# Layer norms finished half by half, second-half transposes inside a product, and reordered queues in both blocks

## The chip, the cores and the metric
One core of a Trainium2 chip runs the whole program in one launch. Its engines are TensorE (PE; matmuls and transposes into PSUM), VectorE (DVE), ScalarE (ACT), GpSimd (POOL) and SyncE (SP, here only the issuer of weight loads). Each takes its instructions in the order in which they were written into its own queue, and waits on semaphores of the others. The metric is the device time of one execution in microseconds. A difference of under 0.2% (3.0 us) is about what a measurement of this kernel can't tell from no change.

## The reference
Activations are [256 tokens, 1024 features], float32. Block 1 has two layers, block 2 has one.
```python
for l in range(2):                                     # block 1
    h = hybrid_mixer(x, ...)                 # attentions A and B, gated unit C, three gates, merge
    x = layer_norm(ALPHA * x + h, ln1_g[l], ln1_b[l])
    h = memory_cross_attention(x, mem, x_wq[l], x_wkv[l], x_wo[l])
    x = layer_norm(ALPHA * x + h, ln2_g[l], ln2_b[l])
    h = conv_ffn(x, ...)                     # (gelu(a) * b) @ w_down, a and b convolved over 3 tokens
    x = layer_norm(ALPHA * x + h, ln3_g[l], ln3_b[l])
def layer_norm(x, g, b):
    mu = jnp.mean(xf, axis=-1, keepdims=True)
    var = jnp.mean(jnp.square(xf - mu), axis=-1, keepdims=True)
    y = (xf - mu) * lax.rsqrt(var + LN_EPS) * g + b
```
Block 2 begins with an RMS norm over the same stream. Then come a gated linear recurrence (LRU) whose gate is gelu(x @ w), attention over compressed, selected and nearby keys, where the compressed keys are `gelu(flat @ w1) @ w2` of overlapping blocks ("phi"), and an MLP.

## The kernel before
The 256 tokens lie as two tiles of 128 (`xt(0)`, `xt(1)`, tile name `xs`), one token in a partition. For a product they are turned by PE to features by tokens: `stream_turned(tag, i, src, need, halves)` writes four 128x128 transposes for each half of the features of tile i (line L596) into a PSUM bank. `stream_split` then takes each half out of PSUM as two fp32r numbers, a high part on ACT (L1082, a cast) and a low part, the residue, on DVE (L1644). Both go to `xTr`. A norm's features, halves and tiles are numbered (i, h) below.

All weights are streamed from `d_wst` by SP (L2550) through a ring of four slots (`raw`). Every piece of 1024 columns is split as well: ACT casts the high part to one of six buffers `wh` (L1061) and DVE subtracts for `lows` (L1625). PE makes three products of a piece (high by high, high by low, low by high; L490), in pieces of two feature rows each, so that a 512-wide product of one token tile has four pieces, a = 0, 2, 4 and 6. Pieces 0 and 2 read the first half of the features, 4 and 6 the second.

The order of each queue is written out by hand: `tensor(e)`, and the functions of ACT and DVE, list what they do in the order in which it stands in the queue. On DVE, `lows_for(..., far=n)` also writes the residues of the next n pieces ahead of what follows it.

A layer norm on DVE adds the residual (L1651), takes moments (L1657, L1662), centres and multiplies with the gain in one instruction over 1024 features (`centred`, L1670), then waits for POOL's inverse root `rs` (L2387) and finishes each half (`rooted`, L1680). After a norm, the next product is made by `tokens_by_tile`: `tile(0)` reads tile 0 while the norm of tile 1 runs, and `tile(1)` follows. There are five such places: `up4` (the feed-forward's first columns) in both layers, `kv` (start of layer 1's mixer, behind layer 0's last norm), `q2` (start of block 2, after the RMS norm, whose halves are already scaled separately, L2010) and `mlp4`. The first norm of each layer has no such product: all 16 transposes stand together, and the next product (`xq`) waits for all four residues (`x_ready`).

Other places that the change touches: `gelu_product` (ACT: gelu of a convolved half L1304, then the high part L1307 of its product `z`, which POOL makes, L2464); the fills of the mixer, in which gate and merge products stand between the steps of the attentions (unit `un` 0 to 7; DVE L1891 mixes v, L1863 is a reciprocal of sums, L1815 multiplies a merged product with its gate); and in block 2 the gates `gelu_gate(n)` with their products `ug`, 112 rows each in a piece of 896 columns, between which stand `phi` (L847, weights read from the ring as they are), its transposes (L862), their copy `hid` (DVE L2109) and the product `cmp` that reads it.

## Time and profile before

| | |
|---|---|
| median of 3 runs | 1511.85 us (1511.59 to 1512.86) |
| time of the profiled execution | 1512.52 us |
| its span | 1510.7 us |
| mean granted TensorE clock | 0.999 of full |
| busy: PE, DVE, ACT, POOL | 98%, 68%, 54%, 15% of the span |
| weights moved | 258.17 MB, mean 171 GB/s |

PE is busy in nearly all of the span, so the table says which engine carries the time, but not what a change next to it costs. For that the timeline is read at each place: when PE starts, what ended its wait, and what stands ahead of the releaser in the queue of its engine.

### The profile page before, as it was taken

Reading aid. Unit: us, or ns where it says so; the run is one execution under the profiler, and the core shown is the slowest. Engines: PE = TensorE matmul, PEld = TensorE weight load, DVE = VectorE, ACT = ScalarE, POOL = GpSimd, SP = SyncE. Lnnn points to the kernel's source line nnn. Section 1 sums busy time; section 2 is a strip of 40 time slices with the busy share of each in tenths; the row PEclk is TensorE's granted clock in tenths of the full one; section 3 lists DMA queues with packets and bytes.
Section 4 is the critical chain, followed back from the end, with each engine's and each line's share of the span. In section 5 each row is a group of like instructions: output and inputs, shape, how many; then the busy total and the mean of one; then the engine's idle time right before and its main releaser. Section 6 shows DMA issues by size and latency. Waiting matters only on the chain.

```text
span 1510.7 us, 24653 instructions
## 1 busy us (share of the span) xinstructions
PE 1484.2 (98%) x10055; PEld 1330.5 (88%) x10055; DVE 1023.1 (68%) x1684; ACT 822.3 (54%) x1453; POOL 228.0 (15%) x190
## 2 busy tenths in 40 slices
PE   9999999999999999999999999999999999999999
PEld 6989879799987899988889998789898999899887
DVE  4865686787856676579578774756685697666743
ACT  5577545466642466654556653355446774455632
POOL 2400132211101230022031110104011142100000
PEclk9999999999999999999999999999999999999999
DMA  8633355455564643355454555556321354555453
GB/s 328 240 132 113 112 195 200 159 187 194 172 223 167 223 140 140 98 182 195 140 194 169 191 188 193 195 183 239 114 61 65 115 192 131 198 195 191 173 195 112
DMA packets 40352, 258.17 MB, mean 171 GB/s; under 512 B 4512, under 2 KB 5168, under 8 KB 14000
## 3 DMA queue, kind: packets, MB, share of 16 engines
q1 hardware_dynamic: 35600, 238.44, 45.1%
q0 software_dynamic: 2272, 12.57, 2.3%
q10 hardware_dynamic: 2368, 5.58, 1.0%
q8 instruction: 80, 1.31, 0.3%
q14 instruction: 32, 0.26, 0.1%
HBM read 254.98 MB, written 1.07 MB: 169 GB/s over the span
## 4 chain that ended last, share of the span: by engine, by line
PE 78%; DVE 12%; ACT 7%; DMA 2%; issue 1%; POOL 1%; SPq 0%; ACTq 0%; POOLq 0%; DVEq 0%
PE ps L490 68%; DVE lows L1625 6%; ACT wh L1061 3%; PE ps L596 3%; PE ps L973 1%; DMA raw<-d_wst 1%; PE ps L679 1%; PE ps L694 1%; PE ps L986 1%; ACT arR L1604 1%; DVE S L2361 1%; ACT S L1168 1%; PE ps L768 1%; ACT S L1260 0%; ACT S L1268 0%
## 5 line engine op out<-in xcount | busy, mean ns | idle before, releaser
L1625 DVE TENSOR_TENSOR lows<-raw,wh 128x1024 fp32r<-128x1024 f32 (+3 forms) x473 | 547.4, 1178 | 253.4 <-ACT wh L1061 252.4
L1061 ACT CAST wh<-raw 128x1024 fp32r<-128x1024 f32 (+3 forms) x473 | 455.3, 989 | 174.6 <-DMA raw<-d_wst 141.4
L490 PE MATMUL ps<-xTr,wh 128*128 128x256 f32 (+2 forms) x3472 | 455.1, 284 | 1.6 <-DVE S L1985 1.6
L490 PEld LDWEIGHTS ps<-xTr,wh 128*128 128x128 f32 (+2 forms) x3472 | 430.3, 190 | 5.2 <-DVE S L1985 3.0
L490 PE MATMUL ps<-wh,arR 128*128 128x512 f32 x928 | 290.1, 397 | 0.0
L490 PE MATMUL ps<-xTr,lows 128*128 128x256 f32 (+1 forms) x1736 | 243.6, 283 | 0.0
L490 PEld LDWEIGHTS ps<-xTr,lows 128*128 128x128 f32 (+1 forms) x1736 | 223.2, 190 | 0.4 <-DVE lows L1625 0.2
L490 PEld LDWEIGHTS ps<-wh,arR 128*128 128x128 f32 x928 | 173.8, 188 | 40.1
L490 PE MATMUL ps<-lows,arR 128*128 128x512 f32 x464 | 182.3, 398 | 4.0 <-DVE lows L1625 4.0
L490 PE MATMUL ps<-wh,xTr 128*128 128x512 f32 x480 | 131.1, 394 | 1.6 <-ACT wh L1061 1.1
L490 PE MATMUL ps<-arR,wh 128*128 128x256 f32 (+1 forms) x832 | 111.9, 281 | 1.4 <-DVE ar L1815 1.4
L490 PEld LDWEIGHTS ps<-lows,arR 128*128 128x128 f32 x464 | 87.4, 188 | 29.2 <-DVE lows L1625 9.0
L490 PEld LDWEIGHTS ps<-wh,xTr 128*128 128x128 f32 x480 | 88.7, 188 | 24.1 <-DVE xTr L1644 2.8
L490 PEld LDWEIGHTS ps<-arR,wh 128*128 128x128 f32 (+1 forms) x832 | 103.6, 188 | 3.4 <-DVE ar L1815 2.3
L2387 POOL TENSOR_TENSOR sm<-sm,cst 128x1 f32<-128x1 f32 (+3 forms) x27 | 44.0, 1629 | 370.1 <-DVE sm L1664 243.5
L490 PE MATMUL ps<-lows,xTr 128*128 128x512 f32 x240 | 74.8, 393 | 0.1
L1325 ACT ACTIVATE S<-ps,ar 128x256 f32<-128x256 f32 x88 | 48.5, 561 | 46.1 <-PE ps L490 46.0
L2464 POOL TENSOR_TENSOR S<-S 128x256 f32<-128x256 f32 x44 | 34.2, 778 | 206.1 <-ACT S L1304 206.1
L490 PE MATMUL ps<-arR,lows 128*128 128x256 f32 (+1 forms) x416 | 62.3, 281 | 0.0
L2452 POOL TENSOR_TENSOR ar<-ar 128x256 f32<-128x256 f32 x32 | 28.4, 899 | 201.5 <-DVE ar L1815 201.5
L490 PEld LDWEIGHTS ps<-arR,lows 128*128 128x128 f32 (+1 forms) x416 | 54.6, 188 | 0.6 <-DVE lows L1625 0.6
L490 PEld LDWEIGHTS ps<-lows,xTr 128*128 128x128 f32 x240 | 44.5, 188 | 11.7 <-DVE lows L1625 2.9
(266 smaller groups left out, 1436.8 us busy)
## 6 DMA issues: line engine op xcount, KB each, us to landing
raw<-d_wst SPq DMA_DIRECT2D x196, 1024.0 KB, 4.8
raw<-d_wst SPq DMA_DIRECT2D x24, 512.0 KB, 3.5
raw<-d_wst SPq DMA_DIRECT2D x12, 896.0 KB, 4.6
raw<-d_wst SPq DMA_DIRECT2D x8, 672.0 KB, 4.6
ar<-d_lnp POOLq DMA_DIRECT2D x5, 1024.0 KB, 5.0
raw<-d_wst SPq DMA_DIRECT2D x8, 441.0 KB, 3.5
ar<-d_par POOLq DMA_DIRECT2D x2, 1192.0 KB, 9.6
ar<-d_scr POOLq DMA_DIRECT2D x1, 2048.0 KB, 9.9
```

What stands on the lines that cost most here:

```text
L490: op = e.matmul(out, s, m, start=start and i == 0, stop=stop and i == len(pairs) - 1)
L596: op = e.transpose(o, x, ident[0:x.shape[0], 0:x.shape[0]])
L679: op = e.matmul(bv[64 * g:64 * g + 64, :, :], va[:, k, v:v + 64], PTv[:, hold + g:hold + g + 3:2, k, :], start=(k == 0), stop=(k == 1))
L694: op = e.matmul(bv[:, k, :], qT[br][lo:lo + 64, 2 * hh + k, i * 128:(i + 1) * 128], kT[br][lo:lo + 64, :], start=True, stop=True)
L768: op = e.matmul(b[:, h * 128:(h + 1) * 128], Vx[:, k, h * 128:(h + 1) * 128], PTv[:, 4 * i + h, k, :], start=(k == 0), stop=(k == 1))
L973: op = e.matmul(b[:, h * 65:(h + 1) * 65], PTv[:, hold + h, k, :], vb[:, k, 4 * br + h, :], start=(k == 0), stop=(k == nkt - 1))
L1061: e.copy(high_of(m), raw_of(m)).then_inc(*high.done(m))
L1325: e.activation(hc[:, s, :], M["up", l, m][:, 0:T], ACT.Identity, bias=cb[:, m:m + 1], scale=ck[:, m, 1:2]).then_inc(*act.done("h", l, m))
L1625: e.tensor_tensor(low_of(m), raw_of(m), high_of(m).bitcast(F32), ALU.subtract).then_inc(*low.done(m))
L2387: return e.tensor_tensor(dst, src, mhalf[0:p, 0:n], ALU.pow)
L2452: e.tensor_tensor(merged[:, d, :], merged[:, d, :], gates[:, gate_at[n] + d, :], ALU.add).then_inc(*pool.done("merged", l, n, d))
L2464: e.tensor_tensor(hc[:, s, :], hc[:, s, :], hc[:, s + 1, :], ALU.mult).then_inc(*pool.done("z", l, n))
```

## The change
The second of the two functions `centred` and `rooted` goes, and so does the first: `scaled_half(tag, i, h)` centres, waits for the root and finishes one half of 512 features, then the other. In the five places that run by tiles, the transposes of tile 1's first half stand before `tile(1)` and those of the second half inside it, before piece a = 4. The feed-forward's `z` parts are written one step later. In the mixer, the mixing of v (unit 0) comes ahead of one more residue, and in unit 7 a gated product comes before the reciprocal. In block 2, one more gate stands between each of phi's steps, and the streamed pieces are grouped accordingly.
```diff
@@ tokens_by_tile
-                def tile(i, turn=None):
+                def tile(i, turn=None, at=6):
                     for a, (x, (wH, wL)) in zip(range(0, 8, 2), xs4):
-                        if turn and a == 6:
+                        if turn and a == at:
                             turn()
@@ up4; the same at kv and, with `scaled`, at q2
                 tile(0)
-                stream_turned(tag, 1, xt(1), normed)
+                stream_turned(tag, 1, xt(1), normed, (0,))
                 product.also("stock", l, 2)
-                tile(1)
+                tile(1, turn=lambda: stream_turned(tag, 1, xt(1), normed, (1,)), at=4)
@@ mlp4
-            tile(0, turn=lambda: stream_turned(tag, 1, xn[1], scaled))
+            tile(0, turn=lambda: stream_turned(tag, 1, xn[1], scaled, (0,)))
             product.also("stock", 2, 2)
-            tile(1)
+            tile(1, turn=lambda: stream_turned(tag, 1, xn[1], scaled, (1,)), at=4)
@@ TensorE, block 2 (ScalarE's and VectorE's queues likewise)
                 if a == 0:
-                    gelu_gate(6)
-                    gelu_gate(7)
-            gelu_gate(8)
+                    for n in range(6, 9):
+                        gelu_gate(n)
+            gelu_gate(9)
...
                 op.then_inc(*cross.done("phT", c))
-            gelu_gate(9)
+            gelu_gate(10)
...
-            for n in range(10, 12):
-                gelu_gate(n)
+            gelu_gate(11)
@@ ScalarE, feed-forward
                                      scale=ck[:, m, 1:2]).then_inc(*act.done("h", l, m))
+                        if n > 1 and half == up_order(n)[0]:
+                            z_high(n - 2)
                     if n:
-                        gelu_product(n - 1)
-                gelu_product(NZ - 1)
+                        gelu(n - 1)
+                gelu(NZ - 1)
+                z_high(NZ - 2)
+                z_high(NZ - 1)
@@ VectorE, norms
-            def centred(tag, i):
-                x = xt(i)
...
-            def rooted(tag, i):
...
+            def scaled_half(tag, i, h):
+                x = xt(i)[:, 512 * h:512 * h + 512]
+                st, mv, nm, ve_, rs, nr = norm_smalls(i)
                 w.wait_ge(ln_in[tag])
+                e.scalar_tensor_tensor(x, x, mv[:, 0:1], lnp[:, 512 * h:512 * h + 512], ALU.subtract,
+                                       ALU.mult).then_inc(*vec.done("gain", *tag, i, h))
+                w.wait_ge(vec, "gain", *tag, i, h)
                 w.wait_ge(pool, "rs", *tag, i)
+                e.scalar_tensor_tensor(x, x, rs, lnp[:, 1024 + 512 * h:1536 + 512 * h], ALU.mult,
+                                       ALU.add).then_inc(*vec.done("ln", *tag, i, h))
@@ VectorE, mixer
                     maxima(un)
+                    if un == 7:
+                        fill(next(todo), far=0)
                     sums(un)
-                    fill_next(2)
+                    fill_next(2 if 0 < un < 7 else 1)
                     if un == 0:
                         mixed()
+                        fill_next(1)
@@ VectorE, block 2
             q_scaled(1)
-            lows_for("ug", 8)
+            lows_for("ug", 8, far=1)
+            lows_for("ug", 9, far=0)
             for c in range(2):
                 w.wait_ge(cross, "phT", c)
                 e.tensor_copy(hid[:, c, :, :], A["phT", c][:, 0:120].rearrange("p (h m) -> p h m", h=2)).then_inc(*vec.done("hid", c))
-            lows_for("ug", 9)
+            lows_for("ug", 10)
```
TensorE's queue at the first by-tile place (`up4`, layer 0), from the last piece of tile(0) to the end of tile(1). Before:
```order
L490 MATMUL ps<-lows,xTr 128x512 x2
L596 MATMUL ps<-cst,xs 128x128 x8
L490 MATMUL ps<-wh,xTr 128x512 x4
L490 MATMUL ps<-lows,xTr 128x512 x2
L490 MATMUL ps<-wh,xTr 128x512 x4
L490 MATMUL ps<-lows,xTr 128x512 x2
L490 MATMUL ps<-wh,xTr 128x512 x4
L490 MATMUL ps<-lows,xTr 128x512 x2
L490 MATMUL ps<-wh,xTr 128x512 x4
```
With the change:
```order
L490 MATMUL ps<-lows,xTr 128x512 x2
L596 MATMUL ps<-cst,xs 128x128 x4
L490 MATMUL ps<-wh,xTr 128x512 x4
L490 MATMUL ps<-lows,xTr 128x512 x2
L490 MATMUL ps<-wh,xTr 128x512 x4
L490 MATMUL ps<-lows,xTr 128x512 x2
L596 MATMUL ps<-cst,xs 128x128 x4
L490 MATMUL ps<-wh,xTr 128x512 x4
L490 MATMUL ps<-lows,xTr 128x512 x2
L490 MATMUL ps<-wh,xTr 128x512 x4
L490 MATMUL ps<-lows,xTr 128x512 x2
```
Eight transposes in one row have become two rows of four, and the second row stands between the second and the third piece of tile(1); nothing else differs here.

VectorE's queue in layer 0's first norm, tile 0 (L1670 is the gain, L1680 the finish). Before:
```order
L1662 BN_AGGR sm<-sm 128x2
L1664 TENSOR_SCALAR sm<-sm 128x1
L1670 SCALAR_TENSOR_TENSOR xs<-xs,sm,ar 128x1024
L1680 SCALAR_TENSOR_TENSOR xs<-xs,sm,ar 128x512 x2
L1625 TENSOR_TENSOR lows<-raw,wh 128x1024 x2
```
With the change (L1676 is now the gain and L1630 the residue of a weight piece):
```order
L1667 BN_AGGR sm<-sm 128x2
L1669 TENSOR_SCALAR sm<-sm 128x1
L1676 SCALAR_TENSOR_TENSOR xs<-xs,sm,ar 128x512
L1680 SCALAR_TENSOR_TENSOR xs<-xs,sm,ar 128x512
L1676 SCALAR_TENSOR_TENSOR xs<-xs,sm,ar 128x512
L1680 SCALAR_TENSOR_TENSOR xs<-xs,sm,ar 128x512
L1630 TENSOR_TENSOR lows<-raw,wh 128x1024 x2
L1656 SCALAR_TENSOR_TENSOR xs<-ps,xs 128x512
```
One instruction over 1024 features is now two over 512, and the second stands behind the finish of the first half, and so behind the wait for POOL's root.

ScalarE's queue in the feed-forward of layer 0 (L1304 gelu, L1307 high part of z, L1325 a product taken out of its bank). Before:
```order
L1307 CAST arR<-S 128x256
L1061 CAST wh<-raw 128x1024
L1325 ACTIVATE S<-ps,ar 128x256 x2
L1304 ACTIVATE S<-S 128x256
L1307 CAST arR<-S 128x256
L1061 CAST wh<-raw 128x1024
```
With the change (gelu L1303, high part of z L1309, out of the bank L1327, weight cast L1060):
```order
L1303 ACTIVATE S<-S 128x256
L1060 CAST wh<-raw 128x1024
L1327 ACTIVATE S<-ps,ar 128x256
L1309 CAST arR<-S 128x256
L1327 ACTIVATE S<-ps,ar 128x256
L1303 ACTIVATE S<-S 128x256
L1060 CAST wh<-raw 128x1024
L1327 ACTIVATE S<-ps,ar 128x256
L1309 CAST arR<-S 128x256
```
The high part of z stood ahead of the next weight cast and of both copies out of PSUM; now it stands behind the cast and one copy, one step later.

## Rows read from the trace of the kernel before
**Rows 1.** The page's part 1: busy us, share of the span, instructions.
```profile
PE 1484.2 (98%) x10055; PEld 1330.5 (88%) x10055; DVE 1023.1 (68%) x1684; ACT 822.3 (54%) x1453; POOL 228.0 (15%) x190
```
**Rows 2.** TensorE's waits: line, releaser, us in total, times, longest.
```profile
PE ps L596 <- DVE xs L1680: 3.7, 3, 1.3
```
**Rows 3.** Timeline (start us, us, what), VectorE, 476 to 483: tile 0's norm.
```profile
477.18 1.27 DVE L1670 SCALAR_TENSOR_TENSOR xs<-xs,sm,ar 128x1024 f32<-128x1024 f32 x1
479.00 1.41 DVE L1680 SCALAR_TENSOR_TENSOR xs<-xs,sm,ar 128x512 f32<-128x512 f32 x2 [0.55 <-POOL sm L2387]
```
**Rows 4.** Timeline, TensorE, 478.5 to 482.5: transposes of a half.
```profile
480.12 0.60 PE L596 MATMUL ps<-cst,xs 128*128 128x128 f32 x4
```
**Rows 5.** Timeline, ScalarE, 476 to 483: the copy of those transposes.
```profile
480.75 0.59 ACT L1082 CAST xTr<-ps 128x512 fp32r<-128x512 f32 x1 [9.65 <-PE ps L596]
```
**Rows 6.** Timeline, VectorE, 485.5 to 492.5: tile 1's norm and residues.
```profile
486.93 1.28 DVE L1670 SCALAR_TENSOR_TENSOR xs<-xs,sm,ar 128x1024 f32<-128x1024 f32 x1
488.25 1.42 DVE L1680 SCALAR_TENSOR_TENSOR xs<-xs,sm,ar 128x512 f32<-128x512 f32 x2
490.36 1.36 DVE L1644 TENSOR_TENSOR xTr<-ps,xTr 128x512 fp32r<-128x512 f32 x2 [0.70 <-ACT xTr L1082]
```
**Rows 7.** Timeline, ScalarE, 488 to 495: both copies of tile 1.
```profile
489.75 1.25 ACT L1082 CAST xTr<-ps 128x512 fp32r<-128x512 f32 x2 [5.37 <-PE ps L596]
```
**Rows 8.** Timeline, TensorE, 487 to 494.5: transposes and products of tile 1.
```profile
489.05 1.32 PE L596 MATMUL ps<-cst,xs 128*128 128x128 f32 x8 [1.25 <-DVE xs L1680]
490.38 1.45 PE L490 MATMUL ps<-wh,xTr 128*128 128x512 f32 x4
...
492.14 1.08 PE L490 MATMUL ps<-wh,xTr 128*128 128x512 f32 x4
```
**Rows 9.** Timeline, TensorE, 966 to 972: the site of q2.
```profile
968.18 1.32 PE L596 MATMUL ps<-cst,PT 128*128 128x128 f32 x8 [0.43 <-DVE PT L2010]
```
**Rows 10.** Timeline, TensorE, 1327 to 1330: the site of mlp4.
```profile
1327.14 1.28 PE L596 MATMUL ps<-cst,PT 128*128 128x128 f32 x8
```
**Rows 11.** Timeline, VectorE, 231 to 241: layer 0's first norm, tile 1.
```profile
234.54 1.41 DVE L1680 SCALAR_TENSOR_TENSOR xs<-xs,sm,ar 128x512 f32<-128x512 f32 x2 [0.52 <-POOL sm L2387]
...
238.15 2.47 DVE L1644 TENSOR_TENSOR xTr<-ps,xTr 128x512 fp32r<-128x512 f32 x4
```
**Rows 12.** Timeline, TensorE, 235 to 242: the first product behind it.
```profile
240.88 1.31 PE L490 MATMUL ps<-xTr,wh 128*128 128x256 f32 x9
```
**Rows 13.** Timeline, ScalarE, 309 to 316: the feed-forward's start.
```profile
310.70 0.41 ACT L1307 CAST arR<-S 128x256 fp32r<-128x256 f32 x1 [0.85 <-POOL S L2464]
```
**Rows 14.** Timeline, TensorE, 312.8 to 315: the same place.
```profile
314.28 0.98 PE L490 MATMUL ps<-xTr,wh 128*128 128x256 f32 x6 [0.82 <-DVE S L1985]
```
**Rows 15.** Timeline, TensorE, 80 to 84: transposes of the mixed v.
```profile
82.13 1.16 PE L596 MATMUL ps<-cst,S 128*128 128x128 f32 x8 [1.11 <-DVE ar L1891]
```
**Rows 16.** Timeline, VectorE, 80 to 84: what stands ahead of them.
```profile
80.16 1.23 DVE L1625 TENSOR_TENSOR lows<-raw,wh 128x1024 fp32r<-128x1024 f32 x1 [1.67 <-ACT wh L1061]
81.30 1.28 DVE L1891 TENSOR_TENSOR ar<-ps,ar 128x512 f32<-128x512 f32 x2
```
**Rows 17.** Busy time, granted clock and DMA share, TensorE, layer 1's same place.
```profile
554.00:558.00 4.00, 4.00 (x21) 0.57 0.00 0
```
**Rows 18.** Timeline, TensorE, 172 to 177.5: the last pv of attention B.
```profile
174.57 1.08 PE L679 MATMUL ps<-PT,ar 128*64 128x256 f32 x8 [1.45 <-DVE ar L1815]
...
176.67 1.10 PE L490 MATMUL ps<-arR,wh 128*128 128x256 f32 x7
```
**Rows 19.** Timeline, VectorE, 171 to 177.5: reciprocal, residues, gated products.
```profile
175.60 0.69 DVE L1625 TENSOR_TENSOR lows<-raw,wh 128x512 fp32r<-128x512 f32 x1 [1.08 <-ACT wh L1061]
```
**Rows 20.** Timeline, TensorE, 1055 to 1062: the compressed keys of block 2.
```profile
1060.98 0.66 PE L490 MATMUL ps<-par,ar 128*60 128x64 f32 x8 [1.53 <-DVE ar L2109]
```
**Rows 21.** Timeline, VectorE, 1055 to 1062: what they wait for.
```profile
1056.57 4.17 DVE L1625 TENSOR_TENSOR lows<-raw,wh 128x896 fp32r<-128x896 f32 x3
```
**Rows 22.** Timeline, SyncE's queue, 1043 to 1056: weights of the gates and phi.
```profile
1043.53 10.24 SPq L2550 DMA_DIRECT2D raw<-d_wst  x5
```

More of the change, by code:

```diff
@@ L804, in tensor @@
                     tile(0)
-                    stream_turned(tag, 1, xt(1), normed)
+                    stream_turned(tag, 1, xt(1), normed, (0,))
                     product.also("stock", l, 3)
-                    tile(1)
+                    tile(1, turn=lambda: stream_turned(tag, 1, xt(1), normed, (1,)), at=4)
             def scaled(i, h):
@@ L816, in tensor @@
             tile(0)
-            stream_turned(tag, 1, xn[1], scaled)
+            stream_turned(tag, 1, xn[1], scaled, (0,))
             product.also("stock", 2, 1)
-            tile(1)
+            tile(1, turn=lambda: stream_turned(tag, 1, xn[1], scaled, (1,)), at=4)
             tokens(("q2", 1), W2, qcols[512:1024], X, [], (act, "q2", 1))
@@ L1034, in tensor @@
             tile = tokens_by_tile(("mlp4",), ("w_mlp_in_2", 0), span(0, 512), tag, (act, "mlp4"))
-            tile(0, turn=lambda: stream_turned(tag, 1, xn[1], scaled))
+            tile(0, turn=lambda: stream_turned(tag, 1, xn[1], scaled, (0,)))
             product.also("stock", 2, 2)
-            tile(1)
+            tile(1, turn=lambda: stream_turned(tag, 1, xn[1], scaled, (1,)), at=4)
             for n in mlp_order:
@@ L1299, in scalar, with gelu @@
                     e.dma_start(PT[:, 0:1024], rel_d).then_inc(*rel_in.done())
-                def gelu_product(n):
+                def gelu(n):
                     s = 2 * n % 8
@@ L1304, in gelu_product, with z_high @@
                     e.activation(hc[:, s, :], hc[:, s, :], ACT.Gelu).then_inc(*act.done("ga", l, n))
+                def z_high(n):
+                    s = 2 * n % 8
                     w.wait_ge(pool, "z", l, n)
@@ L1410, in scalar @@
                 gelu_gate(i)
-            for n in range(2, 8):
+            for n in range(2, 9):
                 gelu_gate(n)
@@ L1417, in scalar @@
                              ACT.Gelu_apprx_tanh).then_inc(*act.done("phi", c))
-            gelu_gate(8)
             gelu_gate(9)
+            gelu_gate(10)
             w.wait_ge(cross, "cmp", 0)
             e.activation(kc2[:, 0:64], A["cmp", 0][0:60, 0:64], ACT.Square, accum_out=kss).then_inc(*act.done("kss"))
-            for n in range(10, 12):
-                gelu_gate(n)
+            gelu_gate(11)
             for i in range(2):
@@ L1664, in averaged @@
                 e.tensor_scalar(ve_, mv[:, 1:2], 1e-5, None, ALU.add).then_inc(*vec.done("var", *tag, i))
-            def centred(tag, i):
-                x = xt(i)
-                mv = list(norm_smalls(i))[1]
+            def scaled_half(tag, i, h):
+                x = xt(i)[:, 512 * h:512 * h + 512]
+                st, mv, nm, ve_, rs, nr = norm_smalls(i)
                 w.wait_ge(ln_in[tag])
-                e.scalar_tensor_tensor(x, x, mv[:, 0:1], lnp[:, 0:1024], ALU.subtract,
-                                       ALU.mult).then_inc(*vec.done("gain", *tag, i))
-            def rooted(tag, i):
-                x = xt(i)
-                rs = list(norm_smalls(i))[4]
-                w.wait_ge(vec, "gain", *tag, i)
+                e.scalar_tensor_tensor(x, x, mv[:, 0:1], lnp[:, 512 * h:512 * h + 512], ALU.subtract,
+                                       ALU.mult).then_inc(*vec.done("gain", *tag, i, h))
+                w.wait_ge(vec, "gain", *tag, i, h)
                 w.wait_ge(pool, "rs", *tag, i)
-                for h in range(2):
-                    c = slice(512 * h, 512 * h + 512)
-                    e.scalar_tensor_tensor(x[:, c], x[:, c], rs, lnp[:, 1024 + 512 * h:1536 + 512 * h], ALU.mult,
-                                           ALU.add).then_inc(*vec.done("ln", *tag, i, h))
+                e.scalar_tensor_tensor(x, x, rs, lnp[:, 1024 + 512 * h:1536 + 512 * h], ALU.mult,
+                                       ALU.add).then_inc(*vec.done("ln", *tag, i, h))
             def gained(tag, i):
                 averaged(tag, i)
-                centred(tag, i)
-                rooted(tag, i)
+                for h in range(2):
+                    scaled_half(tag, i, h)
             def normed(tag, name, scale, i):
@@ L1709, in normed_by_tile @@
                 lows_due(others[2], far=0)
-                centred(tag, 1)
-                rooted(tag, 1)
+                for h in range(2):
+                    scaled_half(tag, 1, h)
                 stream_split(tag, 1)
@@ L1799, in merged_low, with fill @@
                                     ALU.subtract).then_inc(*vec.done("mergedl", l, d))
-                def fill(item):
+                def fill(item, far=NH - 1):
                     kind, n, d = item
@@ L1805, in fill @@
                         return
-                    lows_for("merge", l, n, d, far=NH - 1)
+                    lows_for("merge", l, n, d, far=far)
                     gt = gates[:, gate_at[n] + d, :]
@@ L1986, in vector @@
                                                ALU.add).then_inc(*vec.done("conv", l, m))
-                    if n:
-                        z_low(n - 1)
+                        if n > 1 and half == up_order(n)[0]:
+                            z_low(n - 2)
                     if l == 0 and n == 6:
@@ L1992, in vector @@
                                         ALU.add).then_inc(*vec.done("rel"))
+                z_low(NZ - 2)
                 z_low(NZ - 1)
@@ L2021, in vector @@
             rms_scaled(tag, 0)
-            centred(last, 1)
+            scaled_half(last, 1, 0)
             stream_split(tag, 0)
-            rooted(last, 1)
+            scaled_half(last, 1, 1)
             lows_for("q2", 0, far=0)
@@ L2117, in vector @@
                                        ALU.mult, ALU.mult).then_inc(*vec.done("kc"))
-            lows_for("ug", 11)
             w.wait_ge(cross, "kcT")
```

2 lines of the change are left out of this document (1 added, 1 removed).

## The prediction
> **What bounds the kernel now.** I read the busy shares first: TensorE is busy in 98% of the span, VectorE in 68% [rows 1]. So the time is PE's, and a change here can add or take only PE's waits. The waits of PE by releaser come next: the transposes L596 wait for VectorE's norm for 3.7 us in all, in three waits of at most 1.3 us [rows 2]. Every other releaser that the change touches has one or two waits in that list, of 0.8 to 1.5 us. There is little to win, and the question is what new wait each edit makes. That is read from the timeline, place by place, with what stands ahead of the releaser in its queue. Sums are made against the profiled execution's 1512.52 us, which is 0.67 us above the median of 1511.85 us; I give the result against the median.
>
> **The tile places up4 (twice) and kv.** The one at 489 us shows all three. PE waits 1.25 us for the finished halves, then writes eight transposes from 489.05 [rows 8]. VectorE ends the gain (1.28 us) and the two finishes (1.42 us together) just before [rows 6]. ScalarE's two copies start at 489.75 and take 1.25 us [rows 7]. The product starts at 490.38 [rows 8], right behind the first copy. So the second half's four transposes lie in the time in which PE waits for the first half's copy, and cost nothing.
>
> With the change the gain of one half, about 0.75 us by the 0.71 us of a finish [rows 6], comes before the first finish, in place of 1.28 us: the first half is ready 0.53 us earlier. From this I take 0.35 us, because tile 0's norm grows. There the full gain lay before the wait for POOL's root, which has 0.55 us of idle time behind it [rows 3]; now the second half's gain stands behind that wait and its 0.79 us are added to VectorE's path, of which I count 0.35 for the place where tile 0's residue is needed. Net: tile(1) starts 0.18 us earlier.
>
> The second half's transposes now stand directly ahead of the piece that reads them. From the first transpose to the copy's start is 0.63 us (480.12 to 480.75), the copy takes 0.59 us [rows 4, 5], and the product follows 0.04 us later (489.75 and half of 1.25, then 490.38): 1.26 us in which PE does nothing but four transposes. Then the residue: the first piece of tile(1) takes 1.45 us for four matmuls where the next takes 1.08 us [rows 8], since the low half starts on VectorE at 490.36 [rows 6], behind the copy: 0.37 us more. Together 1.63 us. Minus 0.18: **+1.45 us each, +4.35 us for three**. The bounds of the copy's exposure: nothing, if the wait were hidden (no row has work between these transposes and the piece), and 1.63 us.
>
> **q2 and mlp4.** At q2 the halves are already scaled by themselves, and the wait is 0.43 us [rows 9]; nothing is won on the first half, the second costs 1.63 us, and VectorE pays 0.13 us more for two gains in place of one (two of 0.71 against 1.28 us): **+1.76 us**. At mlp4 all eight transposes stand inside tile(0), 1.28 us without a wait [rows 10]; about 0.6 us of it, four of them, goes, and 1.63 us comes: **+1.05 us**.
>
> **The first norm of each layer.** Nothing is turned by tiles here. After its norm VectorE goes straight on: finish at 234.54, residues of weights, then the four residues of x from 238.15 for 2.47 us, to 240.62; the next product needs all four and starts at 240.88 [rows 11, 12]. The wait for the root is 0.52 us [rows 11]. Each tile's norm grows as above by 0.79 us (0.71 for an instruction behind the root that stood ahead of it, and its issue), so the last residue ends at 242.2, and PE, which had 0.17 us to spare, starts 1.41 us later. **+1.4 us in each layer, +2.8.** It can be nothing if the residues of weights ahead could give way, but they stand in the same queue.
>
> The Trainium skill ("TensorE: Matmul & The Clock Gate", section "Architectural detail") says that the queues of ACT and DVE are strict FIFO. By that rule the second half's gain can't run in the idle time before the root, and these 0.79 us are paid; were it not so, the sum would be 2.8 us less. The trace agrees: VectorE stands idle for 0.52 us before the finish at 234.54 while two ready weight residues are queued behind it [rows 11]. The skill's page "VectorE: DVE Perf Modes" (section "The TRN2 errata") states a fixed cost for each instruction, so that two of 512 cost more than one of 1024; the rows have 1.42 against 1.28 us [rows 6], which is the 0.13 above.
>
> **The feed-forward's start.** ScalarE waits 0.85 us for POOL's z before it casts z and then the next weights [rows 13]. One step later PE waits 0.82 us for the bank that VectorE frees late [rows 14]. With the high part of z behind the cast and one copy, that lateness goes. Waits are booked from a modelled end of the last matmul, and starts are about 0.25 us closer, so I take **−1.07 us in each layer, −2.15**. The bounds are 0 and that.
>
> **Mixer.** In unit 0 of layer 0 the transposes wait 1.11 us [rows 15] for the mixing of v (1.28 us), which stands behind a weight residue of 1.23 us [rows 16]. One residue moves behind it: **−1.15 us**. In layer 1 PE's granted clock is 0.57 at that place (554 to 558) [rows 17] and PE is late itself; nothing is won there. In unit 7 the pv product's wait of 1.45 us goes, but the product at 176.67 [rows 18] waits for the next gated product, which stands behind the residue of 175.60 [rows 19] as before: the wait only moves, **0**, with bounds of −1.4 and 0 in each layer.
>
> **Block 2.** The product cmp waits 1.53 us for the copy hid [rows 20], which stands behind three residues, 4.17 us [rows 21]. With one gate more on PE before it and the copy behind one residue, the wait goes. Against it stands the ring: the weights of these gates and of phi come in five loads over 10.24 us [rows 22], about 2 us each, just in time, and they are grouped anew. I take **−1.4 us** of a possible 1.7 (booked 1.53 and the ends), down to 0.
>
> **Sum.** 4.35 + 1.76 + 1.05 + 2.8 = 9.96 us of cost; 2.15 + 1.15 + 1.4 = 4.70 us of gain: **+5.3 us**. 1512.52 + 5.3 = 1517.8 us profiled, and 1511.85 + 5.3 = **1517.1 us** against the median. The range of this case: without unit 7's extra and with the ring's gain at 0.8 to 1.7 us, and 0.3 us either way at each of five tile places, 1515.0 to 1519.5 us.
>
> **Rivals.**
> *The second half's turn is hidden (the other side).* If PE found the second halves copied in time, for instance because the matmuls queued before piece 4 were still running when ScalarE copied, each place would cost only its transposes, which it also had before. The first halves would then give up to 0.5 us at three places (−0.5 net of tile 0), and if the first norms also cost nothing the gains of 4.70 us stand alone: 1511.85 − 4.7 − 0.5 ≈ 1506.7 us, faster. It decides at the piece a = 4: does it start within 0.1 us of the last transpose? Against it: the piece reads what those transposes write, and the shortest turn in the rows is 1.26 us. Chance 0.10.
> *The first norms cost nothing, or half.* If the residues of x needn't wait, 2.8 us go: 1514.3 us, within 0.2%. Against it: VectorE has no gap but the root's between 231 and 241. With a larger gain of unit 7 (−1.4 each) the same side is reached: 1514.3 us too. Chance 0.20 for both.
> *The ring in block 2 comes late.* The 1.4 us are not won, and one slot late costs about 2 us less the half that lies beside other work: +1.4 to +2.4, 1518.5 to 1519.5 us. For it: five loads just in time. Chance 0.12.
> *The clock.* The stretch at 0.57 in layer 1 [rows 17] stands in an ordinary part of the mixer and may go or move when the work ahead of it shifts: 4 us at 0.57 in place of 1 cost at most 1.7 us, so 1515.4 us if it goes, 1518.8 us if a second comes. Chance 0.08. By itself: the Trainium skill ("TensorE: Matmul & The Clock Gate", Part 1) has only two levels for this clock, and the row's 0.57 is a mean over both.
> *Forecast as summed.* Chance 0.50.
>
> **Numbers.** Slower by over 0.2% (beyond 1514.9 us; 0.2%, 3.0 us, is about what a measurement of this kernel can't tell from no change): the forecast 0.50, the ring 0.12, most of the clock 0.06, 0.68 together. Same: 0.20 and the clock's rest, 0.22. Faster: 0.10. The range leaves out the hidden turn and reaches from 1512.5 (the second rival with 1.8 us to spare, as when both of its mechanisms come in part) to 1520.5 us (the ring's full price and a tile place each 0.2 us dearer).
>
> **What would show it.** Right: after the change, at each by-tile place a second row of four transposes, and behind it PE waits 0.9 us for ScalarE's L1082 or its residue; the first product after the first norm of each layer starts about 1.4 us later after its transposes; no wait for L1985 at 314 and 789 us, for L1891 at 82 us, for hid in block 2. Wrong: the piece a = 4 right behind its transposes; VectorE idle before the residues of x; a new wait of PE for a raw weight slot near 1050 us; pv's wait gone in unit 7 with nothing in its place.

## The result and the profile after

| | before | with the change |
|---|---|---|
| median | 1512.13 us (1511.11 to 1513.51, 12 runs) | 1516.06 us (1515.43 to 1518.99, 12 runs) |
| profiled execution | 1512.52 us | 1515.71 us |
| span | 1510.7 us | 1513.9 us |
| PE busy | 1484.2 us, 98% | 1485.4 us, 98% |

The ratio is 1.0028, 95% interval 1.0020 to 1.0035: slower by 3.9 us, which is more than the 0.2% that can be told from no change. The forecast was +5.3 us, 1517.1 us. Executions far above all others of the same kernel (one of 6013 us in experiment 2, one of 2058 us in experiment 9) are left out of the medians.

TensorE's list of waits, as in [rows 2]: line, releaser, us in total, times, longest.
```profile
PE ps L490 <- ACT xTr L1081: 6.4, 10, 0.7
...
PE ps L596 <- DVE xs L1680: 2.2, 3, 0.7
...
PE ps L596 <- ACT S L1180: 2.0, 2, 1.0
...
PE ps L490 <- ACT ar L1422: 0.9, 1, 0.9
PE ps L490 <- DVE xTr L1649: 0.7, 2, 0.4
```
The first row is new: ten waits for ScalarE's copy of turned features, two at each of the five by-tile places (in the kernel before there was one, of 0.3 us). The wait for finished halves fell from 3.7 to 2.2 us. In place of the pv product's two waits (one is in [rows 18]) there are two for the probabilities (L1180), of 0.98 us in layer 0, and the product behind them still waits 0.47 us for the next gated product (L1815). The waits for phi's copy (L1422) and for the last residue (L1649) are new.

The same by-tile place as in [rows 8], TensorE:
```profile
489.70 0.66 PE L596 MATMUL ps<-cst,xs 128*128 128x128 f32 x4 [0.72 <-DVE xs L1680]
491.03 1.45 PE L490 MATMUL ps<-wh,xTr 128*128 128x512 f32 x4 [0.68 <-ACT xTr L1081]
...
492.77 1.07 PE L490 MATMUL ps<-wh,xTr 128*128 128x512 f32 x4
...
494.14 0.60 PE L596 MATMUL ps<-cst,xs 128*128 128x128 f32 x4
495.41 1.45 PE L490 MATMUL ps<-wh,xTr 128*128 128x512 f32 x4 [0.68 <-ACT xTr L1081]
496.70 0.63 PE L490 MATMUL ps<-lows,xTr 128*128 128x512 f32 x2
```
The wait ahead of the first turn is 0.72 us in place of 1.25, since the first half is ready earlier. From the second turn (494.14) to the product that reads it (495.41) there are 1.27 us, forecast 1.26; and that piece's four matmuls take 1.45 us where those of 492.77 take 1.07, because they wait for the residue too. Both are what the forecast had for the exposed copy.

VectorE in the first norm of layer 0, tile 1, and the product behind it, as in [rows 11, 12]:
```profile
231.76 0.74 DVE L1676 SCALAR_TENSOR_TENSOR xs<-xs,sm,ar 128x512 f32<-128x512 f32 x1
233.02 0.75 DVE L1680 SCALAR_TENSOR_TENSOR xs<-xs,sm,ar 128x512 f32<-128x512 f32 x1 [0.52 <-POOL sm L2391]
...
237.41 2.48 DVE L1649 TENSOR_TENSOR xTr<-ps,xTr 128x512 fp32r<-128x512 f32 x4
```
```profile
240.14 2.03 PE L490 MATMUL ps<-xTr,wh 128*128 128x256 f32 x15 [0.37 <-DVE xTr L1649]
```
The last residue ends at 239.89, and PE waits 0.37 us for it. Here the forecast was wrong: VectorE's idle time before the first finish is still 0.52 us, though the gain ahead of it takes 0.74 us in place of 1.27. The wait was forecast to grow by the difference. GpSimd's root, of the kernel before and of the changed one, tells why:
```profile
232.91 1.52 POOL L2387 TENSOR_TENSOR sm<-sm,cst 128x1 f32<-128x1 f32 x1 [6.96 <-DVE sm L1664]
```
```profile
231.92 0.99 POOL L2391 TENSOR_TENSOR sm<-sm,cst 128x1 f32<-128x1 f32 x1 [7.75 <-DVE sm L1669]
```
It took 1.52 us beside a gain of 1024 features and takes 0.99 us beside one of 512: it got shorter by the same 0.53 us.

**Where the time went, step by step.** Both traces have 10,055 matmuls, in nearly the same order, so the start of the n-th can be compared. The difference (with the change less before, in medians over 24 matmuls) moves only at a few places:

| place | forecast | trace |
|---|---|---|
| unit 0, layer 0 | −1.15 | −1.15 |
| unit 7, both layers | 0 | −0.1, −0.2 |
| first norm, layers 0 and 1 | +1.4, +1.4 | +0.5, +0.5 |
| up4 (layer 0), kv, up4 (layer 1) | +1.45 each | +3.0 (1.6 of it clock), +1.1, +1.2 |
| feed-forward, both layers | −1.07 each | −1.09, −1.04 |
| mixer, layer 1, at the half clock of [rows 17] | 0 | −1.6 (0.4 of it clock) |
| q2 | +1.76 | +1.8 |
| block 2, phi and cmp | −1.4 | +1.1, then −1.8 |
| mlp4 | +1.05 | +1.45 |
| small ones, behind 1230 us | | −0.5 |

The steps add up to 3.2 us, which is the difference of the two spans. What the clock has in a step is told below.

In unit 0 the transposes start at 81.00, right behind PE's own work (in [rows 15] at 82.13 after 1.11 us of waiting), and in the feed-forward the product of [rows 14] follows the transposes of 312.26 after 0.14 us:
```profile
79.93 1.14 PE L694 MATMUL ps<-ar 64*128 64x256 f32 x8
81.00 1.09 PE L596 MATMUL ps<-cst,S 128*128 128x128 f32 x8
```
```profile
312.26 0.38 PE L596 MATMUL ps<-cst,ar 128*128 128x128 f32 x2
312.40 2.16 PE L490 MATMUL ps<-xTr,wh 128*128 128x256 f32 x16
```
The granted clock at these places (window, us, PE busy, clock, DMA share, GB/s):
```profile
293.00:296.00 3.00, 2.33 (x9) 0.85 0.14 22
296.00:299.00 3.00, 3.00 (x10) 0.58 0.87 328
554.00:558.00 4.00, 4.00 (x22) 1.00 0.30 127
```
The stretch at half clock that the kernel before had at 554 to 558 us [rows 17] isn't there; one is at 295 to 299 us, in tile(1) of up4. Each trace has one of 3.4 us, but they don't cost the same. The one in up4 costs 1.6 us. The one in the mixer of layer 1 stood where PE would otherwise have waited for the mixing of v. A kernel with the mixer of before, but without that stretch (experiment 8), shows the wait, and the changed kernel has neither:
```profile
557.72 1.16 PE L596 MATMUL ps<-cst,S 128*128 128x128 f32 x8 [1.09 <-DVE ar L1889]
```
```profile
558.76 1.09 PE L596 MATMUL ps<-cst,S 128*128 128x128 f32 x8
```
By the starts of experiment 8, that kernel gains only 0.4 us where the stretch is gone. So of the −1.6 us in layer 1 about 0.4 us are clock, and about 1.2 us are the reordered mixer, for which the forecast had nothing there.

In block 2, TensorE and ScalarE:
```profile
1054.00 1.10 PE L490 MATMUL ps<-xTr,lows 128*112 128x256 f32 x8
1055.20 3.67 PE L847 MATMUL ps<-raw,S 128*60 128x256 f32 x32
1059.74 2.17 PE L490 MATMUL ps<-xTr,wh 128*112 128x256 f32 x16 [0.87 <-ACT ar L1422]
```
```profile
1058.91 0.78 ACT L1422 ACTIVATE ar<-ps 60x256 f32<-60x256 f32 x2 [0.44 <-PE ps L847]
```
phi's second product starts 0.26 us later than PE could (eight matmuls from 1054.00, 0.12 us apart, end their issue at 1054.94), for its weights, and the gate behind it waits 0.87 us for the copies of phi out of PSUM (two, 0.78 us together). No wait for `hid` is left.

### The profile page after: what moved, and what is told of

It is laid out like the page before. It is cut to its first block, busy times and chain, and to the rows that moved or that the text cites. A ratio compares the mean times of both kernels' runs of the same rounds, so it can differ in the third digit from the quotient of the medians.

```text
span 1513.9 us, 24698 instructions
## 1 busy us (share of the span) xinstructions
PE 1485.4 (98%) x10055; PEld 1329.4 (88%) x10055; DVE 1025.8 (68%) x1696; ACT 821.2 (54%) x1453; POOL 226.0 (15%) x190
## 3 DMA queue, kind: packets, MB, share of 16 engines
HBM read 254.98 MB, written 1.07 MB: 169 GB/s over the span
## 4 chain that ended last, share of the span: by engine, by line
PE 76%; DVE 13%; ACT 7%; issue 2%; DMA 1%; POOL 1%; ACTq 0%; POOLq 0%; DVEq 0%; SPq 0%
PE ps L490 67%; DVE lows L1630 6%; ACT wh L1060 3%; PE ps L596 3%; PE ps L972 1%; PE ps L694 1%; DMA raw<-d_wst 1%; DVE sm L1662 1%; PE ps L985 1%; DVE xs L1680 1%; PE ps L679 1%; DVE xs L1656 1%; ACT arR L1609 1%; DVE S L2365 1%; POOL sm L2391 1%
## 5 line engine op out<-in xcount | busy, mean ns | idle before, releaser
L1630 DVE TENSOR_TENSOR lows<-raw,wh 128x1024 fp32r<-128x1024 f32 (+3 forms) x473 | 546.9, 1177 | 228.4 <-ACT wh L1060 227.7
L1060 ACT CAST wh<-raw 128x1024 fp32r<-128x1024 f32 (+3 forms) x473 | 455.5, 990 | 177.8 <-DMA raw<-d_wst 144.5
L490 PE MATMUL ps<-wh,xTr 128*128 128x512 f32 x480 | 134.4, 399 | 7.7 <-ACT xTr L1081 6.4
L2391 POOL TENSOR_TENSOR sm<-sm,cst 128x1 f32<-128x1 f32 (+3 forms) x27 | 40.6, 1506 | 389.1 <-DVE sm L1669 248.5
L1327 ACT ACTIVATE S<-ps,ar 128x256 f32<-128x256 f32 x88 | 49.4, 565 | 80.3 <-PE ps L490 80.3
L1985 DVE SCALAR_TENSOR_TENSOR S<-ps,ar,S 128x255 f32<-128x255 f32 x88 | 42.4, 481 | 27.2 <-ACT S L1327 27.1
```

What stands on the lines that cost most here:

```text
L490: op = e.matmul(out, s, m, start=start and i == 0, stop=stop and i == len(pairs) - 1)
L1060: e.copy(high_of(m), raw_of(m)).then_inc(*high.done(m))
L1327: e.activation(hc[:, s, :], M["up", l, m][:, 0:T], ACT.Identity, bias=cb[:, m:m + 1], scale=ck[:, m, 1:2]).then_inc(*act.done("h", l, m))
L1630: e.tensor_tensor(low_of(m), raw_of(m), high_of(m).bitcast(F32), ALU.subtract).then_inc(*low.done(m))
L1985: e.scalar_tensor_tensor(h[:, 1:T], b[:, 0:T - 1], ck[:, m, 0:1], h[:, 1:T], ALU.mult, ALU.add).then_inc(*vec.done("conv0", l, m))
L2391: return e.tensor_tensor(dst, src, mhalf[0:p, 0:n], ALU.pow)
```

## The experiments
Each ran beside the kernel before on the same chip, and each ratio is to it there (1511.8 to 1512.2 us). Distances to the changed kernel are to its 1516.06 us above, measured beside 1512.13 us.

**1. The turns back where they were** (norms and all else changed), at all five places; at up4 and kv:
```diff
-                stream_turned(tag, 1, xt(1), normed, (0,))
+                stream_turned(tag, 1, xt(1), normed)
-                tile(1, turn=lambda: stream_turned(tag, 1, xt(1), normed, (1,)), at=4)
+                tile(1)
```


> The changed kernel, with all eight transposes of tile 1 again where they stood before, at all five tile places; everything else stays changed. Theory (a turn directly ahead of the piece that reads it is exposed): 1.27 us of turn and 0.37 us of waiting for the residue go at each place, 1.64 us; at the three layer norms about 0.45 us comes back, because the second half is finished only 1.4 us after the first and its transposes now wait for it; at mlp4 0.35 us for the four transposes. Sum -6.5 us: about 1509.6 where the changed kernel has 1516.1 and the kernel before 1512.1. Rival (the turns are hidden and the loss lies in the halved norms): stays within 1 us of 1516.1.


Measured: 1508.87 us (8 runs), 0.9975 of before (0.9965 to 0.9985). That is 7.2 us below the changed kernel. By the comparison of starts 1.4 us go at kv, 1.4 at up4 in layer 1, 1.8 at q2 and 1.6 at mlp4; at up4 in layer 0 it is 3.0 us, with the half-clock stretch that isn't there in this trace. TensorE at kv:
```profile
486.29 0.66 PE L596 MATMUL ps<-cst,xs 128*128 128x128 f32 x4 [0.71 <-DVE xs L1680]
487.73 0.66 PE L596 MATMUL ps<-cst,xs 128*128 128x128 f32 x4 [0.79 <-DVE xs L1680]
488.15 1.17 PE L490 MATMUL ps<-wh,xTr 128*128 128x512 f32 x4
```
The second turn now waits 0.79 us for its half, and tile(1) starts 0.42 us behind that turn, with no wait for a copy. So the moved turns cost more than the change loses in all; the rest of it is a gain.

**2. The second turn one piece earlier**, `at=2` in place of `at=4` at the five places.


> The changed kernel, with the second half's transposes inside tile(1) one piece earlier, ahead of a = 2 in place of a = 4. Same number of transposes, same halves. Theory (it is the wait for the copy that costs): the piece a = 2 runs 1.38 us on the first half's features while ScalarE copies and VectorE takes the residue, so 0.92 + 0.37 us go at each of the five places, -6.4 us, about 1509.7; no wait of TensorE for the copy behind the second turn. Rival (a turn inside a product costs by its transposes and the switch of operand, wherever it stands): under 1 us won, above 1515.


Measured: 1511.8 us (median of 10 runs), 4.2 us below the changed kernel, against 6.4 expected; ratio to before 0.9997 (0.9988 to 1.0006). TensorE at kv:
```profile
492.87 0.60 PE L596 MATMUL ps<-cst,xs 128*128 128x128 f32 x4
493.22 1.17 PE L490 MATMUL ps<-wh,xTr 128*128 128x512 f32 x4
494.23 0.63 PE L490 MATMUL ps<-lows,xTr 128*128 128x512 f32 x2
494.69 1.07 PE L490 MATMUL ps<-wh,xTr 128*128 128x512 f32 x4
```
The turn costs 0.35 us, the piece after it starts at once, and piece a = 4 (494.69) finds copy and residue: the starts moved by −1.2 us at each place (kv −0.34 and −0.89, up4 of layer 1 −1.26, q2 −1.12 and −0.17, mlp4 −1.28), as expected. The missing 2.2 us lie elsewhere, by all signs in the clock: this trace has three stretches at half clock, where the changed kernel's has one:
```profile
218.00:221.00 3.00, 3.00 (x8) 0.50 0.02 5
295.00:300.00 5.00, 4.59 (x14) 0.66 0.55 192
554.00:559.00 5.00, 5.00 (x26) 0.69 0.02 10
```
The times go with the mean clock that each run reports: 1509.95 us at 0.999 (one run), 1510.75 to 1511.42 at 0.998 (four), 1512.24 to 1513.24 at 0.997 (five). The single run at 0.999 is 5.8 us below the changed kernel's median of its seven at 0.999 (1515.7).

**3. Both gains ahead of both finishes** in tile 0's norms and in the first norm of each layer:
```diff
-                for h in range(2):
-                    scaled_half(tag, i, h)
+                for h in range(2):   # gain of half h
...
+                for h in range(2):   # wait for the root, finish of half h
```


> The changed kernel, with both halves' gains ahead of both finishes in the norms of tile 0 and in the first norm of each layer (at tile 1 of the tile places the order stays). In both kernels VectorE waits 0.52 us for GpSimd's root, though the root took 1.52 us beside a gain of 1024 features and 1.00 us beside one of 512. Theory A (GpSimd's small operation gets through between two instructions of VectorE): root still done 0.4 us after the first gain, no idle time on VectorE, each norm of tile 0 and of the first norms shorter by 0.4 to 0.5 us, and the 0.5 us that TensorE waits for the last residue in each layer goes: -1.0 us, about 1515.1. Theory B (it gets through only when VectorE stands idle): root 1.5 us long again, idle time 0.5 us, 0 +- 0.3 us. Theory C (the root's length is chance): root lengths unrelated to the gains.


Measured: 1514.05 us (11 runs), 2.0 us below the changed kernel against 1.0 expected, ratio 1.0010 (1.0002 to 1.0019). VectorE, and the product behind:
```profile
231.02 1.40 DVE L1690 SCALAR_TENSOR_TENSOR xs<-xs,sm,ar 128x512 f32<-128x512 f32 x2
232.35 1.41 DVE L1696 SCALAR_TENSOR_TENSOR xs<-xs,sm,ar 128x512 f32<-128x512 f32 x2
```
```profile
239.49 1.72 PE L490 MATMUL ps<-xTr,wh 128*128 128x256 f32 x13
```
No idle time is left before the finish, though the second gain started right behind the first: theory A. PE doesn't wait for the residue. The starts show −0.6 us at each first norm and −0.3 at tile 0 of up4 in layer 0; the other 1.6 us in this profile is the half-clock stretch in up4, which it doesn't have.

**4. The gains of experiment 3 in quarters** (256 features).


> The kernel with both gains first (e3), its gains in quarters of 256 features. Theory (GpSimd's root ends 0.4 us after the end of the VectorE instruction that runs when it starts): the first quarter takes about 0.48 us, so the root takes 0.7 to 0.75 us where it took 0.98 beside 512 features and 1.52 beside 1024. Rival (a root has a fixed length of about 1 us in this place and 1.5 was something else): 0.98 us again. VectorE doesn't wait for the root either way.


GpSimd's root:
```profile
232.50 0.72 POOL L2401 TENSOR_TENSOR sm<-sm,cst 128x1 f32<-128x1 f32 x1 [7.54 <-DVE sm L1669]
```
0.72 us, as expected. With 1.52 beside 1.27 us of gain and 0.99 beside 0.74, the root takes the VectorE instruction that runs beside it and 0.25 us. In the kernel before and the changed one VectorE's waiting finish bears out the root's end (it starts 0.11 us behind it); here nothing waits for the root, so 0.72 us rests on its own record. The kernel's one time was 1513.76 us; its starts are level with experiment 3's but for a half-clock stretch at 79 to 83 us.

**5. The changed kernel with the norms of before** (gain over 1024 features).


> The changed kernel with only the norms as before (one gain over 1024 features). Theory (halving is nearly neutral, since GpSimd's root gets shorter with the gain that it runs beside): the 0.5 us of TensorE's wait at the first norm goes in each layer, and the first halves at up4, up4 and kv come 0.3 us later: -0.1 +- 0.5 us, 1516.0. Rival (the forecast's own step: 0.79 us for each norm, 1.4 us in each layer): -2.8 us at the first norms, 1513.5 or less. Root 1.52 us long again at 224 and 233 us by the theory.


Measured: 1517.14 us (5 runs, 1.0031, 1.0019 to 1.0043). That is 1.1 us above the changed kernel; its trace has two half-clock stretches. The starts, with the stretches taken off: −0.5 us at each first norm, −0.3 at tile 0 of up4 in layer 0, and +0.5 to +0.6 us at tile(1) of each of up4, kv and up4; the root takes 1.52 us again. So the halved norms cost 1.0 us at the first norms and give somewhat more than that back at the three by-tile places. The forecast's 2.8 us for them were wrong.

**6. Only the moved turns**, in the kernel before.


> The kernel before, with only the second half's transposes moved inside tile(1) ahead of a = 4 at the five places (norms and queues as before). Theory: +1.64 us at up4, up4, kv and q2 less what the first half's copy is waited for anyway (0), +1.3 at mlp4: +7.9 us, 1520.0 against 1512.1. Rival (part of the loss needs the halved norms, which this kernel hasn't): +4 us or less.


Measured: 1524.14 us, 1.0077 (1.0064 to 1.0091): +12.1 us, far beyond both expectations. The starts move by 3.2 us at each of up4, kv and up4, and by 1.7 and 1.4 at q2 and mlp4. The last two are the expected 1.64 and 1.3. The first three have 1.6 us more each, and there the clock is (a fourth stretch is at 78 us):
```profile
297.00:300.00 3.00, 3.00 (x10) 0.54 0.70 292
495.00:498.00 3.00, 3.00 (x9) 0.55 0.80 322
777.00:780.00 3.00, 3.00 (x9) 0.60 0.74 268
```
The first of them starts at 296.3 us, behind two waits:
```profile
293.77 0.66 PE L596 MATMUL ps<-cst,xs 128*128 128x128 f32 x4 [1.26 <-DVE xs L1680]
295.10 1.54 PE L490 MATMUL ps<-wh,xTr 128*128 128x512 f32 x4 [0.67 <-ACT xTr L1082]
```
The wait for the second turn's copy comes after the fall (301.08). The stretches don't come in every execution: one of the four runs took 1521.68 us at a mean clock of 0.999, the others 1524.06 to 1524.74 us at 0.997 and 0.995.

**7. The same with idle matmuls** in the two waits ahead of tile(1), at those three places:
```diff
                 tile(0)
+                warm(1)
                 stream_turned(tag, 1, xt(1), normed, (0,))
+                warm(1)
```


> The kernel before with only the moved transposes (1524.1, whose trace has three half-clock stretches of 3.4 us right behind tile(1)'s start at up4, kv, up4), and one more idle matmul (0.87 us at full clock, its result unused) in each of the two waits ahead of tile(1) at these three places. Theory (TensorE's thin use there drops the clock, which costs 1.6 us a place): no stretch at half clock at the three places, 4.8 us less in a profile that had all three, 1519.5. Rival (the clock falls for reasons elsewhere): stretches at the same three places, 1524 or a little more.


Measured: 1520.58 us (5 runs, 1.0059, 1.0046 to 1.0073), 3.6 us faster than experiment 6, though it does more; 1519.5 us was expected.
```profile
297.00:300.00 3.00, 2.33 (x13) 1.00 0.90 328
495.00:498.00 3.00, 2.33 (x12) 1.00 0.82 273
777.00:780.00 3.00, 2.32 (x12) 1.00 0.92 287
```
All three stretches are gone; the one stretch of this trace is at 558 us, in the mixer. So PE's thin use there (in experiment 6 two waits in a row, of 1.26 and 0.67 us) let the clock fall, and the filled waits keep it up. The Trainium skill ("TensorE: Matmul & The Clock Gate", "HAM oscillation") tells of longer pauses, waits for DMA between bursts of matmuls, that bring the lower level back. The traces agree as to the cause, with shorter waits and 1.6 us lost at each place.

Each side is one trace, but the other traces fit. Without idle matmuls, kernels with the moved turns have a stretch at one of these places in the changed kernel and in experiments 2, 5 and 9, and none in 3 and 4; the five traces of kernels without the moved turns have none there. Waits aren't the only cause: stretches at 78 to 79 us and at 551 to 559 us come in kernels of both kinds, and PE is busy in all of [rows 17]. Why they come there wasn't tried.

**8. Only block 2's part**, in the kernel before.


> The kernel before with only block 2's part of the change. Theory: the 1.6 us of cmp's wait go, 0.87 us for phi's bank and 0.26 us for phi's weights come, -0.5 us, 1511.6. Rival (the forecast's step): -1.4, 1510.7. The trace separates them better than the times: TensorE's steps at 1052 to 1061 us.


Measured: 1510.97 us (10 runs) against 1511.81 (0.9993, 0.9984 to 1.0002): −0.8 us, which the interval doesn't tell from none. The starts show +1.0 us behind phi, then −1.6 and −0.2 at cmp: −0.8.

**9. The changed kernel with gate 8 behind phi's second product**:
```diff
-                    for n in range(6, 9):
+                    for n in range(6, 8):
                         gelu_gate(n)
+            gelu_gate(8)
             gelu_gate(9)
```


> The changed kernel, with one gate (8) back behind phi's second product, so that two gates stand between phi's products in place of three; then gates 8 and 9, the transposes, gate 10, cmp, gate 11. In the changed kernel the product behind phi waits 0.87 us for ScalarE to copy phi out of PSUM, and phi itself 0.26 us for its weights. Theory (four banks: with three gates between, the next product gets phi's own bank; with two it doesn't): both waits go, -1.1 us, 1515.0 where the changed kernel has 1516.1; no wait for the copy of hid either. Rival (the wait is for ScalarE being late, whatever the bank): the wait for the same copy stays, 1516.


Measured: 1515.7 us (median of 7 runs; 1.0026, 1.0015 to 1.0036) against 1515.0 expected: at most 0.4 us faster than the changed kernel, which the interval doesn't tell from none.
```profile
1052.15 3.67 PE L847 MATMUL ps<-raw,S 128*60 128x256 f32 x32
1055.95 2.12 PE L490 MATMUL ps<-xTr,wh 128*112 128x256 f32 x16
...
1061.46 1.20 PE L490 MATMUL ps<-xTr,lows 128*112 128x256 f32 x8 [0.57 <-DVE lows L1632]
```
The gate behind phi (1055.95) no longer waits for the copies, and phi doesn't wait for weights: the bank was the cause. But gate 9 now waits 0.57 us for its residue, which on VectorE's queue stands behind the scaling of q and starts at 1059.78, and of 1.06 us won 0.8 us are lost again.

**10. Three waits only**: the kernel before with the feed-forward's and the mixer's part, and in block 2 no regrouping but
```diff
-            lows_for("ug", 8)
+            lows_for("ug", 8, far=1)
```


> The kernel before, with only three parts: the feed-forward's z one step later, the mixer's reordered fills, and in block 2 no regrouped gates but the copy hid behind one weight residue in place of three (residues limited to one piece ahead there). Norms and transposes as before. Theory: -2.15 for the feed-forward, -1.15 for unit 0, -1.6 for hid, since the product that reads it could start at 1059.3 and the copy would be done there: 1507.2 against 1512.1, and TensorE has no wait for the copy out of phi's bank. Rival (the residues pushed back make a new wait of the next gate): hid gives 0 to -0.6, about 1508.5. The half-clock stretch may move either by 1.6 us.


Measured: 1508.14 us (7 runs), 0.9977 (0.9966 to 0.9988): 4.0 us below the kernel before, where 4.9 were expected. The steps of its trace, a run of 1507.04 us, add up to 5.5 us; its other runs have mean clocks of 0.997 and 0.998, and one has 0.947 and took 1511.87 us.
```profile
1052.26 2.17 PE L490 MATMUL ps<-xTr,wh 128*112 128x256 f32 x16
1054.36 1.20 PE L490 MATMUL ps<-xTr,lows 128*112 128x256 f32 x8
1055.48 0.66 PE L490 MATMUL ps<-par,ar 128*60 128x64 f32 x8
```
The product cmp (1055.48) follows the gate without a wait, −1.58 us by the starts, for one argument changed. Unit 0 gives −1.27, unit 7 −0.4 and −0.1, the feed-forward −1.11 and −1.08.

**11. The same with the norms by halves**, both gains first (experiment 3), turns as before.


> The three waits' version (d1), with the norms by halves too: both gains ahead of both finishes in tile 0's norms and the first norms, gain and finish half by half at tile 1 of the tile places; transposes as in the kernel before. Theory: nothing at the first norms (VectorE's path gets 0.45 us per tile shorter, TensorE wasn't waiting there), and 0.3 to 0.6 us at each of up4, up4 and kv, since the first halves are ready 0.5 us earlier and tile 0's residues too: -1.2 us against d1's 1508.1, 1506.9. Rival: the second halves come 0.2 us later than before, their transposes stand ahead of tile(1) and take it all back: 1508 or more. No run with three half-clock stretches is meant by these numbers; each adds about 1.5 us.


Measured: 1507.02 us (6 runs), 0.9965 (0.9953 to 0.9977); the fastest kernel of the study, 5.0 us below the kernel before. The starts show −0.3 us at up4, at kv and at up4, as expected; the first norms nothing. Its trace has three half-clock stretches; its one run at a mean clock of 1.000 took 1505.16 us. Against experiment 10 the 1.1 us lie within both intervals.

## Why the prediction was right, and where it was off
The sign and the main mechanism held, and the time lies in the range. That it came as near is in part luck, since misses of both signs stand against each other (sum below). **The exposed turn** is right to 0.02 us (1.27 us, and 1.45 against 1.07 for the piece; the 0.04 us between copy and product go with a copy of 0.59 us, and with half of 1.25 us there is no gap, which leaves the sum), shown by undoing it (7.2 us back) and by moving it one piece earlier (1.2 us back at each place). The rival of a hidden turn is refuted by the same two. **q2** is right. **mlp4** came to +1.45 us in place of +1.05: four transposes less save 0.64 us in tile(0), as assumed, but the product behind them runs into a wait for a weight residue (0.21 us as booked), and the next piece starts 0.48 us later than it could. **up4 and kv** came to +1.1 us at kv, +1.2 at up4 in layer 1 and, with the clock taken off, +1.4 at up4 in layer 0, in place of +1.45 each. The forecast took 0.35 us off the 0.53 us by which the first half is ready earlier, for the growth of tile 0's norm; by the starts of the first turn the whole 0.53 us are won at kv and at up4 in layer 1, and 0.27 us at up4 in layer 0.

**The first norms** are the failed term: "Each tile's norm grows as above by 0.79 us", +1.4 us in each layer. The order of VectorE's queue was read rightly, and so was its idle time before the root in the kernel before, but the root's own time was taken as fixed from the end of the variance. It isn't: it ends 0.4 us after whichever VectorE instruction ran at its start (experiments 3 to 5). So the half's gain brought the root forward by 0.53 us, and a norm grew by 0.25 us only. The term was +0.5 us in each layer. The 0.17 us that PE was said to have to spare there aren't in the rows either: with the change the product starts 0.25 us behind the last residue, and in the kernel before it was 0.26 us.

**Feed-forward and unit 0** are right to 0.1 us. **Unit 7** was put at 0 and gave 0.1 and 0.2 (0.4 and 0.1 in experiment 10). The wait moved, but only 0.47 us of it to the next gated product, as said; the longer part, 0.98 us, is for the probabilities (L1180), which the forecast hadn't. **Unit 0 of layer 1** was put at nothing, since PE was late by its clock. That held for that trace only: without the stretch the reordering gives about 1.2 us there too.

**Block 2** was put at −1.4 us and came to −0.7. The wait for `hid` went as said. The risk was sought in the ring, which cost 0.26 us; what was missed is the bank. phi and the gates share four banks in turn, and a third gate between phi's halves gives phi's own bank to the product right behind it.

**The clock** was a rival at 0.08, as a loss or gain of one stretch. The stretch of [rows 17] went, which by itself gave 0.4 us, and another came in up4, which cost 1.6 us. The sum didn't move by luck: the difference is the 1.2 us of unit 0 in layer 1. What the forecast didn't see is that the waits it added can bring such stretches themselves: experiment 6 had three, at 1.6 us each.

Sum of the misses: −1.8 (first norms), −0.7 (up4, kv), +0.4 (mlp4), +0.7 (block 2), −0.3 (unit 7), −0.5 (small ones, not explained), +0.1 (q2), and +1.2 for the clock against −1.2 for unit 0 in layer 1, make −2.1, and 5.3 − 2.1 = 3.2 us, as in the two profiles. The medians differ by 3.9 us. The mean clock of the changed kernel's runs is 0.998 or 0.997 in five of twelve, and those took 1516.85 to 1518.99 us, so more stretches in some runs are likely in the other 0.7 us; no trace of those runs is at hand.

## What to carry to other kernels
A transpose that stands right ahead of the product that reads it costs the whole round through the copy (here 1.27 + 0.37 us for 0.35 us of transposes); one piece of other work in between hides it, and a wait that is there anyway hides it for nothing. Before a product is put behind another in a ring of banks, count which bank it gets; the added third gate cost 0.87 us. A wait can be shortened by what is put beside it: order and size of VectorE's instructions set when GpSimd's small one ends.

## What the runs showed of the hardware that was not expected
- GpSimd's root of one number in each partition takes 0.72, 0.99 and 1.52 us beside VectorE instructions over 256, 512 and 1024 features, and needs no idle VectorE afterwards: the next gain may start at once (experiment 3). The Trainium skill ("VectorE: DVE Perf Modes", "Two Vector instructions with no wait between them") says that VectorE reads the second of two SBUF inputs through an interface that is shared with GpSimd; the gain has two such inputs, and these lengths fit with that, but what holds GpSimd back wasn't tried apart.
- Two waits in a row, of 1.26 and 0.67 us, brought TensorE from 2.4 to 1.2 GHz for a stretch at three of three places in one trace and cost 1.6 us each beyond themselves; with an idle matmul in each wait no stretch came there (experiments 6 and 7). A stretch cost only 0.4 us where PE would have waited for VectorE anyway (experiment 8).
- Runs of one kernel at mean clocks of 0.999, 0.998 and 0.997 had median times of 1509.95, 1511.05 and 1512.70 us (experiment 2), steps as large as what most single edits here are worth. In experiment 10 the order is less clear.
